# Last LayerNorm of a two-layer diffusion trunk: the normalised tile in PSUM, and the next tile's statistics ahead of the wait for this tile's root

## The reference, cut to what matters

```python
def layer_norm(x, g, b):
    xf = x.astype(F32)
    mu = jnp.mean(xf, -1, keepdims=True)
    var = jnp.mean(jnp.square(xf - mu), -1, keepdims=True)
    return ((xf - mu) * lax.rsqrt(var + LN_EPS) * g.astype(F32) + b.astype(F32)).astype(x.dtype)
...
            h = layer_norm(DN_ALPHA * h + g2 * ec_moe(u, moe_router[l], moe_w1[l], moe_w3[l], moe_w2[l]),
                           ln_g[l, 1], ln_b[l, 1])
    return h, hgrn_states, ret_states
```

## Time and profile before

| | us |
|---|---|
| median of 3 runs | 4527.57 |
| the profiled execution, its own time | 4524.45 |
| its span, first to last instruction | 4522.7 |
| TensorE busy | 4240.8 (94%) |
| VectorE busy | 1269.4 (28%) |
| ScalarE busy | 674.3 (15%) |
| GpSimd busy | 239.8 (5%) |

### The profile page before, as it was taken

The page is one execution under the profiler, slowest core; times in us unless marked ns, Lnnn a source line. Parts: engine busy times, 40 slices in busy tenths (PEclk is TensorE's granted clock), DMA queues, the critical chain, the costliest instruction groups (busy, mean ns, idle before and its releaser), DMA issues. The chain is left out here.

```text
span 4522.7 us, 61624 instructions
## 1 busy us (share of the span) xinstructions
PE 4240.8 (94%) x26949; PEld 3690.0 (82%) x26949; DVE 1269.4 (28%) x3047; ACT 674.3 (15%) x1675; POOL 239.8 (5%) x132
## 2 busy tenths in 40 slices
PE   8799988999968999999998999999968999999995
PEld 4577775577438999999998888888538999999995
DVE  6424452254380000000001453442580000000003
ACT  0122221100221110101101311111221110110111
POOL 0000000000210000000000300000210000000001
PEclk8999999999989999999999999999989999999998
DMA  7410001031326788878786201000426777777775
GB/s 287 152 44 26 22 4 33 24 138 59 120 86 240 292 305 290 305 284 311 279 298 239 84 29 45 26 24 20 154 88 219 274 280 280 277 273 281 276 278 203
DMA packets 147414, 785.39 MB, mean 174 GB/s; under 512 B 14792, under 2 KB 51304, under 8 KB 101258
## 3 DMA queue, kind: packets, MB, share of 16 engines
q1 hardware_dynamic: 137930, 747.89, 44.6%
q0 software_dynamic: 9216, 33.56, 3.5%
HBM read 725.20 MB, written 56.20 MB: 173 GB/s over the span
## 5 line engine op out<-in xcount | busy, mean ns | idle before, releaser
L1749 PE MATMUL PS<-arena 128*128 128x144 f32 x11264 | 1441.9, 287 | 7.0 <-ACT arena L1784 6.5
L1749 PEld LDWEIGHTS PS<-arena 128*128 128x128 f32 x11264 | 1406.9, 190 | 8.1 <-ACT arena L1784 7.3
L1734 PE MATMUL PS<-arena 128*128 128x144 f32 x5632 | 743.4, 286 | 0.0
L1734 PEld LDWEIGHTS PS<-arena 128*128 128x128 f32 x5632 | 711.3, 190 | 4.5 <-issue 4.5
L1842 DVE TENSOR_TENSOR arena<-PS,arena 128x144 f32<-128x144 f32 x352 | 108.4, 308 | 2005.4 <-ACT arena L1810 2005.4
L1810 ACT ACTIVATE arena<-PS 128x144 f32<-128x144 f32 x352 | 102.5, 291 | 1716.0 <-PE PS L1749 1716.0
L2222 PE MATMUL PS<-arena 128*128 128x256 f32 x1152 | 259.5, 384 | 11.0 <-DVEq L2549 11.0
L1385 PE MATMUL PS<-arena 128*128 128x512 f32 x576 | 259.3, 605 | 5.3 <-PEq L2592 4.8
L2174 PE MATMUL PS<-arena 128*128 128x256 f32 x1152 | 253.2, 380 | 1.7 <-ACT arena L2390 1.7
L2222 PEld LDWEIGHTS PS<-arena 128*128 128x128 f32 x1152 | 219.7, 193 | 41.5 <-issue 12.1
L2174 PEld LDWEIGHTS PS<-arena 128*128 128x128 f32 x1152 | 218.3, 191 | 31.9 <-issue 2.8
(11 more groups left out here) (330 smaller groups left out, 3341.6 us busy)
## 6 DMA issues: line engine op xcount, KB each, us to landing
arena<-expert_panels SPq DMA_DIRECT2D x352, 1536.0 KB
arena<-ada_w SPq DMA_DIRECT2D x6, 4096.0 KB, 14.0
arena<-ada_w SPq DMA_DIRECT2D x12, 2048.0 KB
arena<-odd_w_in SPq DMA_DIRECT2D x16, 1024.0 KB, 5.7
arena<-hgrn_w SPq DMA_DIRECT2D x20, 512.0 KB, 4.0
arena<-filter_spectra SPq DMA_DIRECT2D x36, 256.0 KB, 2.7
mid_rows<-arena SPq DMA_DIRECT2D x18, 512.0 KB, 2.9
filter_spectra<-arena SPq DMA_DIRECT2D x16, 512.0 KB, 3.8
```

The source lines that it names most:

```text
L1734: m = pe.matmul(PS[:, m_ // 3, m_ % 3 * SLOTS:m_ % 3 * SLOTS + SLOTS], s.w2[n % RING][:, m_ * P:(m_ + 1) * P], s.hid[:, f, :], start=f == ...
L1749: m = pe.matmul(PS[:, 6 + n % 2, q * 256:q * 256 + SLOTS], s.w13[n % RING][:, q, k, :], s.xs[e % 2][:, k, :], start=k == 0, stop=k == KD - 1)
```

## The change

1. ScalarE writes the normalised tile into one of two PSUM buffers `n` (banks 0 and 1, or 2 and 3) instead of the SBUF buffer `o`. VectorE's product reads it there and writes `o` in SBUF; the product of the last turn stays in PSUM, and the last addition reads it there and writes `o`. The wait for an earlier store of `o` moves from ScalarE's norm to VectorE's product.
2. On VectorE the statistics of turn i+1 stand ahead of the wait for the root of turn i (before, the statistics of turn i+1 stood behind the product of turn i-1). On ScalarE the root of turn i+1 stands ahead of the norm of turn i. There are three small buffers `st` for the statistics in place of two.

The lists of SP and GpSimd keep their instructions and waits.

```diff
@@ -1867,7 +1867,8 @@
                 s.l, s.yc, s.scattered = l, yc, scattered
                 s.y = [at(base + b * D, D) for b in range(3)]
                 s.o = [at(base + 3072 + b * D, D) for b in range(3)]
-                s.st = [at(base + 6144 + 24 * b, 24) for b in range(2)]
+                s.st = [at(base + 6144 + 24 * b, 24) for b in range(3)]
+                s.n = [PS[:, 2 * b:2 * b + 2, :].rearrange("p a b -> p (a b)") for b in range(2)]
                 s.ln = at(lnrows, 2, D)
                 sm = lambda n: sem(f"me_{n}")
                 s.yl, s.sv = [sm(f"sum_in{b}") for b in range(3)], [sm(f"stored{b}") for b in range(3)]
@@ -1903,30 +1904,42 @@
                 pass
 
             def act(s, act, ch):
+                for i in range(NT + 1):
+                    if i < NT:
+                        st = s.st[i % 3]
+                        act.wait_ge(s.var, i + 1)
+                        act.activation(st[:, 15:16], st[:, 14:15], ACT.Sqrt).then_inc(s.sd, 1)
+                    if i:
+                        st = s.st[(i - 1) % 3]
+                        if i >= 3:
+                            act.wait_ge(s.mg, i - 2)
+                        act.wait_ge(s.sc, i)
+                        act.activation(s.n[(i - 1) % 2], s.source(i - 1), ACT.Identity, bias=st[:, 17:18],
+                                       scale=st[:, 16:17]).then_inc(s.na, 1)
+
+            def stats(s, dve, ch, i):
+                st, x = s.st[i % 3], s.source(i)
+                if i:
+                    dve.wait_ge(s.yl[(i - 1) % 3], 16 * ((i - 1) // 3 + 1))
+                for n in range(2):
+                    m = dve.bn_stats(st[:, 6 * n:6 * n + 6], x[:, n * 512:n * 512 + 512])
+                ch.link(m)
+                ch.link(dve.bn_aggr(st[:, 12:14], st[:, 0:12]))
+                dve.tensor_scalar(st[:, 14:15], st[:, 13:14], EPS, None, ALU.add).then_inc(s.var, 1)
+
+            def gain(s, dve, i):
+                out = s.o[i % 3] if i < NT - 1 else s.n[i % 2]
+                dve.wait_ge(s.na, i + 1)
+                if 3 <= i < NT - 1:
+                    dve.wait_ge(s.sv[i % 3], 16 * (i // 3))
+                dve.tensor_tensor(out, s.n[i % 2], s.ln[:, 0, :], ALU.mult).then_inc(s.mg, 1)
+
+            def dve(s, dve, ch):
+                s.stats(dve, ch, 0)
                 for i in range(NT):
-                    st = s.st[i % 2]
-                    act.wait_ge(s.var, i + 1)
-                    act.activation(st[:, 15:16], st[:, 14:15], ACT.Sqrt).then_inc(s.sd, 1)
-                    if i >= 3:
-                        act.wait_ge(s.sv[i % 3], 16 * (i // 3))
-                    act.wait_ge(s.sc, i + 1)
-                    act.activation(s.o[i % 3], s.source(i), ACT.Identity, bias=st[:, 17:18],
-                                   scale=st[:, 16:17]).then_inc(s.na, 1)
-
-            def gain(s, dve, i):
-                dve.wait_ge(s.na, i + 1)
-                return dve.tensor_tensor(s.o[i % 3], s.o[i % 3], s.ln[:, 0, :], ALU.mult).then_inc(s.mg, 1)
-
-            def dve(s, dve, ch):
-                for i in range(NT):
-                    st, x = s.st[i % 2], s.source(i)
-                    if i:
-                        dve.wait_ge(s.yl[(i - 1) % 3], 16 * ((i - 1) // 3 + 1))
-                    for n in range(2):
-                        m = dve.bn_stats(st[:, 6 * n:6 * n + 6], x[:, n * 512:n * 512 + 512])
-                    ch.link(m)
-                    ch.link(dve.bn_aggr(st[:, 12:14], st[:, 0:12]))
-                    dve.tensor_scalar(st[:, 14:15], st[:, 13:14], EPS, None, ALU.add).then_inc(s.var, 1)
+                    st = s.st[i % 3]
+                    if i + 1 < NT:
+                        s.stats(dve, ch, i + 1)
                     dve.wait_ge(s.sd, i + 1)
                     ch.link(dve.reciprocal(st[:, 16:17], st[:, 15:16]))
                     dve.scalar_tensor_tensor(st[:, 17:18], st[:, 12:13], -1.0, st[:, 16:17], ALU.mult,
@@ -1935,8 +1948,8 @@
                         s.gain(dve, i - 1)
                 s.gain(dve, NT - 1)
                 dve.wait_ge(s.mg, NT)
-                o = s.o[(NT - 1) % 3]
-                dve.tensor_tensor(o, o, s.ln[:, 1, :], ALU.add).then_inc(s.last, 1)
+                dve.wait_ge(s.sv[(NT - 1) % 3], 16 * ((NT - 1) // 3))
+                dve.tensor_tensor(s.o[(NT - 1) % 3], s.n[(NT - 1) % 2], s.ln[:, 1, :], ALU.add).then_inc(s.last, 1)
 
             def pool(s, pool):
                 for i in range(NT - 1):
```

## The result

The changed kernel takes 4536.84 us (median of 22 runs, 4531.56 to 4543.0), the kernel before 4528.01 us in 22 runs beside it. The ratio is 1.0019, with a 95% interval of 1.0013 to 1.0026: 8.8 us by the medians, 8.6 us by the ratio. The forecast was +9.6 us and 4537.1 us.

The account below looks back on a forecast made before the run. The prediction took GpSimd's addition plus VectorE's next product, through the held shift, as the bound, with loads nearly touching. Terms 1.74 + 9.37 - 1.5 = +9.6 us on 4527.57 gave 4537.1 us, range 4533.0 to 4539.8.

Parts of the forecast that it names:

- The bound of before: Steady turns: GpSimd's addition holds VectorE's shift, so a turn is addition plus next product, 3.57 us.
- PSUM gives turns 0 to 7 nothing: Product from PSUM: the shift ahead of it, inputs in SBUF, is still held by GpSimd's addition, so no gain.
- Start, +1.74: Up to turn 0's product: reciprocal and shift now stand behind turn 1's statistics, which wait for the first load; +1.74 us.
- Pairs, +9.37: Products 0 to 6: statistics wait for loads of turns 4, 6, 8; pairs take 10.29 us, before 7.17; +9.37 us.
- End, -1.5: After product 6: last product no longer held, saving 2.05 us, but the last two stores overlap; -1.5 us.
- Rival, the last shift ahead of GpSimd: End: turn 8's shift starts before GpSimd's addition and is not held; -1.0 us, so +8.6 us in all; chance 0.22.
- Rival, faster loads: Pairs: loads land sooner on an emptier queue; +8.4 us in all, or 4534.2 us by the skill's formula; chance 0.13.
- PSUM against SBUF: Products and norm: PSUM costs the same as SBUF, 0 us; the skill's table would add 0.065 us a product.
- The sum: Whole changed stage: start, pairs and end together, +9.6 us.
- The side that had been given 0.58: Whole kernel: slower by over 0.2%, beyond the line of 9.05 us; chance 0.58.

Follow-up runs that it names:

- e1: The changed kernel with the old order of statistics and root put back, product still from PSUM; ratio 0.9999 to the kernel before.
- e7: The kernel before with the shift -mean/sd as a one-tensor tensor_scalar with a pointer to 1/sd; ratio 1.0001 to the kernel before.
- e9: The changed kernel with all loads issued first, the tensor_scalar shift, and turn 0's scale and shift ahead of turn 1's statistics; ratio 0.9993 to before.
- e10: The kernel of e9 with the product in place in SBUF again; ratio 1.0001 to the kernel before.
- e2: The changed kernel without PSUM, product in place in SBUF, new order kept; ratio 1.0023 to the kernel before.
- e4: The changed kernel with eight load buffers and all loads issued at the start of the stage; ratio 1.0002 to the kernel before.
- e3: The changed kernel with SP's load moved ahead of the wait for GpSimd's addition and of the store; ratio 1.0002 to the kernel before.
- e6: The changed kernel with the shift -mean/sd as a one-tensor tensor_scalar with a pointer to 1/sd; ratio 1.0022 to the kernel before.
- e11: The kernel of e9 with the order of statistics and root of the kernel before; ratio 1.0001 to the kernel before.
- e8: The kernel before with eight load buffers and all loads issued at the start of the stage; ratio 0.9999 to the kernel before.
- e13: The kernel of e9 with the bias of turn 7 added by VectorE out of PSUM, not by GpSimd; 4523.65 us, ratio 0.9988 to before.

## Why the prediction was right

- **The bound of before** (addition plus product, through the held shift, 3.57 us a turn). Shown: e1 leaves B unchanged though the product is free; e7 passes the hold on; e9, with neither held and the new order, drops to 3.08; e10 brings it back.
- **PSUM gives turns 0 to 7 nothing.** Right: e1.
- **Start, +1.74.** Measured +1.19. The first load happened to land after 3.5 us rather than 3.8, and the reciprocal no longer waits for anything just before it and begins 0.08 us before the instruction ahead has ended, where I had it begin 0.02 us after. The first 0.34 us are scatter of a landing, the other 0.21 such overlaps that I had left out. In e2 to e4, with the first load at 3.5 to 3.8, it is +1.30 to +1.55.
- **Pairs, +9.37.** Measured +9.09. VectorE waits for the loads of turns 4, 6 and 8 for 3.44, 3.49 and 3.50 us (the brackets), 10.4 us together, and another 0.5 us for those of turns 5 and 7. That is more than the growth, since the waits for the root, 0.27 us in each of these six turns before, are gone. Shown to be the place of the load in SP's list: e3 undoes it with that one move, and e2 has it without PSUM.
- **End, -1.5.** Measured 10.61 us against 11.65, so -1.0. The mis-sized term is the last store: I took 3.05 us, halfway between 2.6 and 3.5, and it took 3.5. The upper bound that I had reckoned for it, 3.5, was the right one.
- **Rival, the last shift ahead of GpSimd.** It did not happen, by 0.02 us, here and in e2, e3 and e4 (shift 2.33 us each time). What it would have been worth was shown by e6, where C fell by 2.1 and the stage by 1.1 us; I had reckoned 1.0.
- **Rival, faster loads.** Landings behind a store stayed at 4.1 and 4.2 us for the loads of turns 4, 6 and 8. They were faster in e3, where no store goes out just ahead of them. The formula that the rival takes from the Trainium skill, "DMA: Bandwidth & Descriptors", is a fit to transfers issued by GpSimd; these go out from SP.
- **PSUM against SBUF.** VectorE's products took 1.21 to 1.23 us from PSUM as from SBUF, so the row of before was the right guide, and the extra 0.065 us, estimated from the Trainium skill's table ("VectorE: DVE Perf Modes", errata table), does not appear. ScalarE's norm into PSUM took 1.21 us for 1.24, a gain of 0.03 us; the Trainium skill, "ScalarE: Activation LUTs", section "Step-by-step: what each stage is for", says that ScalarE writes faster to PSUM than to SBUF, and the trace agrees.

The sum was 0.4 us above the stage's 9.24. That is closer than its terms: start and pairs were 0.8 us too high, the end 0.5 us too low, and part of this cancelled. The measured ratio, 1.0019, lies at the line of 0.2% where the forecast put it, and its interval reaches to both sides of it: the forecast lay 0.5 us above the line, the measurement 0.4 us below. The side that had been given 0.58 did not come, and an interval as wide as this one does not tell the two sides apart.

## What to carry to other kernels

An instruction moved ahead on an in-order engine takes its waits with it: before moving it, follow what it waits for back to the issue, here a load that stood behind a store, behind an addition, behind a product. When instructions of two engines hold each other up, look for the small instruction that is held, not only for the large one; freeing the large one gives nothing while the small one stands ahead of it. An idea can be sound (2.1 us in the stage, e9 against e11) and lose five times that where another bound is next (10.4 us, the change against e1). One move in SP's list took this loss away (e3), but nothing was gained until the shift and the product were freed as well (e9).

## What was not expected of the hardware

- A load of 512 KB issued 0.38 us behind a store landed after 3.9 to 4.3 us in the kernel before and the change, and after up to 5.0 us in e2; with the last store 1.3 us or more ahead it landed after 3.4 to 3.8 us (e3).
- The first store behind a queue of eight loads took 5.9 us to land in e8 (issued 9.6 us after the first load), 5.1 in e11 (9.7 us after it), and 3.4 to 4.0 us in e4, e9, e10 and e13 (11.0 us or more after it). Stores with no other transfer near them took 2.6 us in the change.
- The one-column `tensor_scalar` with a pointer takes 0.21 us against 0.16 for the `scalar_tensor_tensor`, but it was not held beside GpSimd in any run (212 to 215 ns over nine in e9, and the same in e6, e7 and e11, where the other took up to 2329 ns in the change). Operation and operand form changed together, so which of the two frees it is open.
